# A hybrid decoder layer on one Trainium2 core: modulation and the first seven projection units in slices of 256 features, seven PSUM banks open at once

## The reference

```python
mod = silu(c) @ w_ada + b_ada                       # w_ada: 1024 x 6144
shift1, scale1, gate1, shift2, scale2, gate2 = split(mod, 6)
h = rms_norm(x, norm1_g) * (1 + scale1) + shift1    # x: 512 x 1024
q, k, v, qi, ki, wi, u, g_attn, g_pool = split_cols(h @ w_in, IN_SIZES)
iscore = sum_over_4_heads(relu(qi @ ki.T) * wi)     # causal
sel = top_k(iscore, 128)                            # per query
attn = softmax(q @ k.T * scale - alibi, over sel) @ v
y_pool = (per group: trailing mean of u over 2, 4, 8, 16 tokens - u) @ w_grp ...
x = x + gate1 * ((sig(g_attn)*(attn @ w_attn_br) + sig(g_pool)*y_pool) @ w_out)
h2 = modulate(x, norm2_g, shift2, scale2)
x = x + gate2 * conv_ffn(h2)
```

## Time and profile before

| | |
|---|---|
| median of 3 runs | 754.99 us (754.11 to 756.42) |
| profiled execution | 759.15 us, of which the span of the trace is 757.2 us |
| PE busy | 739.7 us, 98% of the span |
| DVE, ACT, POOL busy | 379.0, 306.6, 312.3 us |
| DMA | 92.75 MB |

### The profile page before, as it was taken

The page is one execution under the profiler, slowest core; times in us unless marked ns, Lnnn a source line. Parts: engine busy times, 40 slices in busy tenths (PEclk is TensorE's granted clock), DMA queues, the critical chain, the costliest instruction groups (busy, mean ns, idle before and its releaser), DMA issues.

```text
span 757.2 us, 9497 instructions
## 1 busy us (share of the span) xinstructions
PE 739.7 (98%) x3568; PEld 597.2 (79%) x3568; DVE 379.0 (50%) x693; ACT 306.6 (40%) x501; POOL 312.3 (41%) x165
## 2 busy tenths in 40 slices
PE   4989999999999999999999999999999999999997
PEld 3467788888777777887899888888788888888886
DVE  2588699972446551774685435464443433004002
ACT  4224513256756763334455343434334343212120
POOL 1125338562623332547423444444444444443431
PEclk9969989999999999999999999999999999999999
DMA  8995511221113113644338344323323321233301
GB/s 327 381 338 204 187 55 57 71 97 56 57 57 112 57 56 107 262 159 128 97 95 267 112 111 112 91 76 112 101 68 110 111 99 68 84 112 112 137 2 56
DMA packets 83995, 92.75 MB, mean 122 GB/s; under 512 B 2035, under 2 KB 66287, under 8 KB 83951
## 3 DMA queue, kind: packets, MB, share of 16 engines
q1 hardware_dynamic: 82719, 87.43, 35.6%
q10 hardware_dynamic: 1232, 4.72, 1.7%
HBM read 90.05 MB, written 2.10 MB: 122 GB/s over the span
## 4 chain that ended last, share of the span: by engine, by line
PE 96%; DVE 1%; DMA 1%; ACT 1%; SPq 0%; issue 0%; DVEq 0%; ACTq 0%
PE bank L1471 42%; PE bank L1491 21%; PE bank L1480 21%; PE bank L1547 2%; PE bank L1741 1%; PE bank L1719 1%; PE bank L1707 1%; PE bank L1513 1%; PE bank L1625 1%; DMA xtok<-in_x_dram 1%; PE bank L1565 1%; PE bank L1614 1%; ACT junk L747 1%; PE bank L1518 1%; PE bank L1775 1%; PE bank L1532 0%
## 5 line engine op out<-in xcount | busy, mean ns | idle before, releaser
L650 POOL TENSOR_TENSOR wsplit<-stage,wsplit 128x1024 fp32r<-128x1024 f32 (+1 forms) x120 | 275.0, 2295 | 395.2 <-ACT wsplit L732 391.7
L1471 PE MATMUL bank<-hT,wsplit 128*128 128x512 f32 (+1 forms) x1264 | 295.3, 386 | 0.0
L1471 PEld LDWEIGHTS bank<-hT,wsplit 128*128 128x128 f32 x1264 | 231.8, 190 | 46.5 <-issue 0.9
L732 ACT ACTIVATE wsplit<-stage 128x1024 fp32r<-128x1024 f32 (+1 forms) x120 | 119.8, 1000 | 280.9 <-PE bank L1480 196.7
L1480 PE MATMUL bank<-hT,wsplit 128*128 128x512 f32 (+1 forms) x632 | 152.8, 384 | 0.0
L1480 PEld LDWEIGHTS bank<-hT,wsplit 128*128 128x128 f32 x632 | 114.7, 188 | 23.5 <-issue 0.8
L1491 PE MATMUL bank<-wsplit,guT 128*128 128x512 f32 x528 | 119.8, 389 | 0.0
L1491 PEld LDWEIGHTS bank<-wsplit,guT 128*128 128x128 f32 x528 | 99.1, 188 | 20.5
L1429 DVE SCALAR_TENSOR_TENSOR yb<-bank,conv,yb 128x511 f32<-128x511 f32 (+1 forms) x44 | 32.9, 749 | 65.1 <-ACT yb L1022 64.3
L1429 DVE SCALAR_TENSOR_TENSOR ya<-bank,conv,ya 128x511 f32<-128x511 f32 (+1 forms) x44 | 33.0, 749 | 59.2 <-ACT ya L1022 58.4
L1364 DVE TENSOR_TENSOR tmp_last<-bank,gate_row 128x512 f32<-128x512 f32 x8 | 5.5, 688 | 101.7 <-PE bank L1491 101.7
(11 more groups left out here) (188 smaller groups left out, 731.8 us busy)
## 6 DMA issues: line engine op xcount, KB each, us to landing
stage<-in_w_up_dram SPq DMA_DIRECT2D x44, 512.0 KB, 5.2
stage<-in_w_in_dram SPq DMA_DIRECT2D x17, 1024.0 KB, 5.3
stage<-in_w_down_dram SPq DMA_DIRECT2D x10, 1024.0 KB, 5.0
ada_early<-in_w_ada_dram SPq DMA_DIRECT2D x8, 1024.0 KB, 10.1
ada<-in_w_ada_dram SPq DMA_DIRECT2D x7, 1024.0 KB, 11.7
ada_mid<-in_w_ada_dram ACTq DMA_DIRECT2D x4, 1024.0 KB, 8.1
stage<-in_w_out_dram SPq DMA_DIRECT2D x4, 1024.0 KB, 6.1
ada_last<-in_w_ada_dram SPq DMA_DIRECT2D x4, 1024.0 KB, 11.1
```

Of the source, the lines that this page charges most:

```text
L650: pool.tensor_tensor(unit_split(n, 1), unit_source(n), unit_split(n, 0).bitcast(F32), ALU.subtract).then_inc(low, 1)
L732: me.did(act.activation(unit_split(n, 0), unit_source(n), ACT.Copy), high)
L1471: pe.matmul(out_bank[:, tokens], hi[:, k, :], rhs[:, part, k, tokens], start=k == 0 and part == 0, stop=False)
```

## The change

- **Modulation 1 by slices.** w_ada's columns for shift1 and scale1 are loaded in four slices q of 256 features (two blocks). PE sums both at once: the lhs is `cpad`, silu(c) in column 0 of 32 columns (the rest zero), and four matmuls of one slice go to four column groups of the array (`first_sums`, 8 matmuls of 128x32 by 128x512). ACT copies the bank out, four matmuls turn it into columns (`first_columns`), DVE adds bias and gain (`first_vectors`).
- **Norm by tile of 128 tokens.** For each tile of x, as it lands: ACT square sum and root, DVE reciprocal and scaling (xn), PE transposes into all eight banks, ACT and DVE copy out once. The diagonal is gone.
- **First seven units at once.** Weights of qi, kw and q come by slices of two feature blocks (896 columns), split per block (high on ACT, low on DVE, not POOL). PE goes block by block over seven open banks, 21 matmuls a block, as hT's blocks become ready.
- **Order** of the units behind: v, u, k instead of u, v, k. The index scores lie among v0 to v2. POOL's low parts reach u2 before the first window sum.
- **shift2, scale2** are summed on DVE during the attention (one row after each odd step t below 16 and from 21 to 35), from two buffers of one row that SP loads between filler items; their column sums lie at step 18 and behind ab1.
- **Small loads** (c, vectors, taps: 12 transfers) are issued by ACT instead of SP.

The core of the diff (the same functions of ACT and SP follow it):

```diff
+    def first(self):
+        for q in range(KQ):
+            self.items.append(("first", "in", (C_Q, C_QI), 2 * q, 2 * q + 2, 1))
...
-    for kind, n in (("qi", 2), ("kw", 1), ("q", KA), ("u", KA), ("v", KA)):
+    s.first()
+    for kind, n in (("v", KA), ("u", KA)):
...
+            def first_sums(q):
...
+                for half in range(2):
+                    pe.wait_ge(ada_in[q][half], 32)
+                    for g in range(KQ):
+                        k = half * KQ + g
+                        mm = pe.matmul(OB[32 * g:32 * (g + 1), :], cpad[:, k, :], ada_first[q][:, k, :],
+                                       start=half == 0, stop=half == 1)
+                mm.then_inc(sums_ok, 1)
...
+            first_sums(0)
+            first_columns(0)
+            for n in range(2):
+                pe.wait_ge(x_kept[n], KD // 2)
+            for k in range(KD - 1):
+                first_products(k, h_hi, 0, 0, start=k == 0)
+                if k % 2:
+                    first_columns(k // 2 + 1)
+                first_products(k, h_lo, 1, 0)
+                first_products(k, h_hi, 0, 1).then_inc(used, 1)
+                if k % 2 == 0 and k < KD - 2:
+                    first_sums(k // 2 + 1)
...
-            top_rounds(4)
+            top_rounds(3)
             pool_mean(0)
-            mod_vector(3)
             top_rounds(2)
             pool_mean(1)
-            mod_vector(4)
-            top_rounds(2)
+            top_rounds(1)
             pool_mean(2)
             top_rounds(2)
             pool_mean(3)
-            top_rounds(3)
...
+                if t % 2 and t < 2 * KD:
+                    mod_row_of(3, t // 2)
+                if t == 19:
+                    mod_vector(3)
+                if t % 2 and 20 <= t < 20 + 2 * KD:
+                    mod_row_of(4, (t - 20) // 2)
```

More of the change, by code:

```diff
@@ L138, in split @@
             self.unit[name] = len(self.units) - 1
+    def first(self):
+        for q in range(KQ):
+            self.items.append(("first", "in", (C_Q, C_QI), 2 * q, 2 * q + 2, 1))
+            self.last_use.append(None)
+            for r in range(2):
+                self.units.append((1, r, KS))
+                self.house()
+                self.item_of.append(q)
+                self.last_use[q] = ("unit", len(self.units))
+        for at, name in enumerate(FIRST):
+            self.opens(name, "dve", at)
+        self.ring = NBANK - 1
     def block_rows(self, w, k0, k1, half, home=None):
@@ L484, in await_chunk @@
         def await_chunk(eng, name):
-            eng.wait_ge(used, sch.unit[name] + 1)
+            if name not in FIRST:
+                eng.wait_ge(used, sch.unit[name] + 1)
+            elif name == FIRST[-1]:
+                eng.wait_ge(used, KD)
+            else:
+                eng.wait_ge(first_ok, FIRST.index(name) + 1)
         def await_drained(eng, name):
@@ L513, in unit_source @@
             slot = stage[:, item % NSTAGE, :]
+            if columns == KS:
+                return slot[:, part * KS:(part + 1) * KS].rearrange("p (k n) -> p k n", n=KS)
             if columns == S:
@@ L540, in load_item @@
                 slot = stage[:, n % NSTAGE, :]
-                _, w, columns, k0, k1, chunks = item
+                kind, w, columns, k0, k1, chunks = item
+                if kind == "first":
+                    for c0, wide, c in FIRST_COLUMNS:
+                        sp.dma_start(slot[:, 0:2 * KS].rearrange("p (k n) -> p k n", n=KS)[:, :, c:c + wide],
+                                     weights[w][:, k0:k1, c0:c0 + wide]).then_inc(stage_in[n % NSTAGE], 16)
+                    return
                 if len(columns) == 2:
@@ L754, in _ @@
[L754 to L765 removed]
+                me.settle()
@@ L1135, in norm, with low_parts @@
-            def norm():
-                dve.wait_ge(root_b, 1)
-                me.settle()
-                def low_part(k):
-                    dve.wait_ge(h_hi, k + 1)
-                    me.did(dve.scalar_tensor_tensor(
-                        out=hT[:, 1, k, :], in0=nrm[:, k % 2, :], scalar=mod[:, k:k + 1],
-                        in1=hT[:, 0, k, :].bitcast(F32), op0=ALU.add, op1=ALU.subtract), h_lo)
-                for k in range(KD):
+            lowered = [0]
+            def low_parts(upto):
+                while lowered[0] < upto:
+                    n = lowered[0]
+                    dve.wait_ge(high, n + 1)
+                    if unit_before(n) is not None:
+                        dve.wait_ge(used, unit_before(n) + 1)
+                    me.did(dve.tensor_tensor(unit_split(n, 1), unit_source(n), unit_split(n, 0).bitcast(F32),
+                                             ALU.subtract), low)
+                    lowered[0] += 1
@@ L1464, in _, with high_products @@
         def _(pe):
-            def high_products(n, out_bank, rhs, tokens=slice(0, S)):
+            def high_products(n, out_bank, rhs, tokens=slice(0, S), blocks=None):
                 hi = unit_split(n, 0)
                 pe.wait_ge(high, n + 1)
-                for k in range(sch.units[n][0]):
+                for k in blocks or range(sch.units[n][0]):
                     for part in range(2):
@@ new lines, in first_columns, with first_products @@
+            def first_columns(q):
+                pe.wait_ge(row_ok, q + 1)
+                for n in range(4):
+                    mm = pe.matmul(OB[:, MC + n:MC + n + 1], rowsum[:, n * P:(n + 1) * P], ones[:, 0:1],
+                                   start=True, stop=True)
+                mm.then_inc(col_ok, 1)
+            def first_products(k, made, part, a, names=FIRST, start=False, stop=False):
+                pe.wait_ge(made, k + 1)
+                pe.wait_ge((high, low)[a], k + 1)
+                for name in names:
+                    at = FIRST_AT[FIRST.index(name)]
+                    mm = pe.matmul(bank(name)[:, :], unit_split(k, a)[:, 0, at:at + P], hT[:, part, k, :],
+                                   start=start, stop=stop)
+                return mm
@@ L1596, in wi_turn, with gate_sums @@
+            def gate_sums(j, n):
+                pe.wait_ge(mod_sum, KD * (ROW_TURN[j] + 1))
+                if n == 0:
+                    pe.wait_ge(mod_ok, ROW_TURN[4] + 1)
+                for half in range(2):
+                    pe.matmul(gate_banks(n)[half][:, :], ones[:, :], macc[:, half * S:(half + 1) * S],
+                              start=True, stop=True).then_inc(gate_sum, 1)
             def wi_turn():
```

502 lines of the change are left out of this document (237 added, 265 removed).

## The result

The kernel after takes **766.06 us** (median of 4 runs, 763.09 to 767.82) where the kernel before took 755.7 beside it (754.11 to 758.38): a ratio of 1.0131, 95% interval 1.0096 to 1.0165. A second series gave 766.8 against 756.29, ratio 1.0129 (1.0100 to 1.0157). It is slower by 1.3%, where 0.6% faster was forecast. The ten runs of the kernel after in the two series spread by 0.7% (762.98 to 768.13), more than the 0.3% named at the top.

The account below looks back on a forecast made before the run. PE was taken as the bound, 96% of the span. Gains of 13.4 (start), 2.9, 3.85 and 0.2, less 9 (wait), 2.9 (clock) and 3.85 (moved sums), gave 4.6 won: median 750.5 us, range 741 to 763.

Parts of the forecast that it names:

- rival B: Column groups in first_sums don't overlap four ways: 770 us if serial, 757 if two ways; chance 0.12.
- part 5: Costs given back in the attention: column sums 3.85 us on PE, row sums on DVE 0, SP's queue 0.
- a new wait of PE in the attention: Sign in the attention: the forecast expected no new PE wait there.
- Parts 1 and 2: Way to the first product, at 23 us, then seven units paced by PE, ending at 70.6; 13.4 us won.
- E: Time at which the first seven units on PE all end, forecast at 70.6 us.
- The low clock: PE at its lower clock: 2 us in the first products, 2.9 us behind the wait for the top k.
- rival E: A later start, from small loads landing behind x or a longer low clock: 4 to 6 us, 755 us; chance 0.10.
- Part 4: DVE's top k comes too late: DVE idles 7 us before the first pooled mean, PE waits 9 us (5.5 to 11).
- the upper bound of E + 100: Latest forecast end of DVE's top-k chain through mean, root and first spread, ahead of kroot's turn; E + 98 taken.
- the low end of the sum (E + 94.6): Earliest forecast end of that same DVE chain ahead of kroot's turn; E + 98 taken.
- Rival D: Row sums on DVE in the attention delay logits: 3 to 8 us, 756 us; chance 0.15.
- Rival C: The top k is on time, with neither wait nor clock loss: 11.9 us better, 739 us; chance 0.13.

Follow-up runs that it names:

- rows_later: Kernel after, with the loads of rows 2 to 15 one filler item later on SP's queue: 763.34 us, ratio 1.0089 to the kernel before.
- start_reordered: Kernel after, with seven small loads moved from ACT to SP and the vectors' rows turned and copied behind most turns of xn: 761.38 us, ratio 1.0069.
- the first profile: Kernel after, unchanged, its first profiled execution, the fastest of its four runs: 763.09 us, span 761.3.
- rows_narrow: Kernel after, with 14 of DVE's 16 row sums in the attention on 128 of 1024 columns, loads and waits kept: 763.58 us, ratio 1.0100.
- second profile: Kernel after, unchanged, profiled once more later: 768.13 us for that execution, span 766.4; series median 766.80 us, ratio 1.0129.
- the best version: The kernel named stat_before_last_round: 747.97 us, ratio 0.9885 to the kernel before.
- stat_before_last_round: Kernel after, with later row loads, reordered top k and start, and q's and k's statistics ahead of the last top-k round: 747.97 us, ratio 0.9885.
- stat_and_busy: As stat_before_last_round, with 30 turns of the identity added on PE at the start: 748.01 us, ratio 0.9889.

## Why the prediction was wrong

- **The bound, and what each sum costs: right.** `first_sums` takes 1.92 us against 1.9, so four column groups do run at once (rival B falls). The moved column sums cost 1.84 each.
- **The step that failed: part 5, SP's queue, "an item is needed four steps or more after that, against a landing of some 5 us, so 0".** It measured 4.6 us, and a new wait of PE in the attention, which the prediction had named as a sign against it, was there with 2.66. ACT had nothing else to do from 198.09 and was waiting for this item, and it landed 6.6 us after its issue, not 5. I counted the distance from the item to its use in steps of the attention, as for a later item; the first item behind rows 2 and 3 could only go when the attention had already begun, because the rows wait for its steps 1 and 3. rows_later removes it whole.
- **Parts 1 and 2: E at 70.6, mis-sized by 1.8 to 5.6.** First product at 25.15 and 26.18 instead of 23: I had put xn behind the fourth root, and it stood behind the rows' landing, their turns and DVE's copies (start_reordered, together with the split of the loads that won nothing by itself: first product at 21.65). The low clock had 2 us in the sum; the 21 first products alone took 0.3 us over their 4.76 (21 x 5.44/24) in the first profile and 3.0 in the second. This was rival E, given 0.10.
- **Part 4: the mechanism right, the size missed, and the wait hit by luck.** DVE's idle 6.91 (forecast 7). But the turn came at E + 101.8 and E + 103.0, over the upper bound of E + 100. Against the low end of the sum (E + 94.6) the first profile is 7.2 late: 1.5 of it was there at the first mean, and some 6 came in the pooled means, which took 13.6 us where the low end has 7.4. PE waited 6.05 + 2.54 + 0.69 = 9.3 us (forecast 9): DVE's chain was 3.8 later than taken, and PE was later too, 2.9 of it by the low clock, which the sum had put behind the wait. The wait's larger part stood ahead of the third k product and not of the turn: I had named `mixed(2)` and missed that `mixed(0)` is late too. The low clock was priced once at 2.9. It came after each wait: 2.9 at 147.14 (6.67 in place of 3.79), 0.9 at the turn (1.97 in place of 1.03) and 0.5 behind it. Against E + 100.9, the forecast with the low clock in it, the turn came 0.9 and 2.1 us late, the score 1.35 and 1.5 later after the turn. The slow DVE operations did come, in the pooled means and not in the mask (0.90 + 1.49, the cheap end): a subtraction of 7 columns took 2.32 us at 131.30, beside a low part of POOL from 131.21 to 133.60, where the kernel before took 0.17 for it with POOL idle. That it was POOL is likely (the last section has the times) but not shown: no run took POOL's work away.
- **Rival D fell**: row sums beside logits cost nothing (rows_narrow against rows_later). Rival C too: the top k was late.
- **The sum.** Its last step is 0.2 off (754.5 - 4.2 is 750.3, not 750.5), which changes nothing. The start was to win 13.4 us and won 7.8 (second profile) to 11.6 (first). Of the 13.8 us between forecast and second profile, 5.6 are the start, 3.6 the way through the top k and 4.6 SP's queue: 4.6 won as forecast became 9.2 lost (766.4 against 757.2). None of the three alone would have made the sign right.

## What to carry to other kernels

A load put on a shared queue costs what stands behind it: where it waits for an engine, find the next entry, who is idle for it and since when, and compare issue times, not steps. When one engine is late, list every bank and buffer that it hands back in order, since the first of them and not the last makes PE wait, and cheap steps (a reciprocal, a drain) can be pulled ahead of long loops. And price a pause of PE as the pause and a low clock that may follow it, each time, with a bound for either case, and take a second profile when the first lies at the edge of its runs.

## What the runs showed of the hardware

- PE work that nothing reads made the kernel faster: 46 turns in idle time took 0.4% off, with 4.11 instead of 5.14 to 6.50 us for the 32 turns of xn. The gain is partly given back later, and with the best version (30 turns) there was none.
- After pauses of 6.05, 5.3 and 2.66 us PE's next matmuls ran at about half pace: sixteen in 6.67 us, eight turns in 1.97, eight matmuls in 3.68. After the pause of 1.19 us in rows_narrow eight matmuls took 2.11, the full pace. The price is not fixed: after a pause of 6.03 us in start_reordered sixteen took 5.37, and after one of 2.29 us sixteen took 3.94 in stat_before_last_round and 5.29 in stat_and_busy.
- DVE took longer where POOL was at work: the same subtraction of 7 columns took 2.32 us beside POOL and 0.17 with POOL idle. It ended at 133.62, where POOL's operation ended at 133.60; a product of 15 columns (1.23 us) ended at 142.92, POOL's at 142.90; in the kernel before one of 2.36 us ended at 139.74, POOL's at 139.71. No run changed POOL's work, so this is read from the times alone.
- Sixteen records of 512 columns in four groups of 32 columns take 1.92 us, where one after the other they would take 6.8 (the estimate of the prediction): a factor of 3.5.
